# A gather that fetches four experts for 32 tokens each, summed in four 32-column groups of TensorE

## The reference

```
def block(xb):                                   # 128 tokens
    q = (xb @ w_pq).reshape(PEER_BLOCK, 8, 2, 128)
    s1 = einsum('thk,nk->thn', q[:, :, 0], sub_keys1)
    s2 = einsum('thk,nk->thn', q[:, :, 1], sub_keys2)
    v1, i1 = top_k(s1, 16);  v2, i2 = top_k(s2, 16)
    cand = v1[..., :, None] + v2[..., None, :]
    sc, ci = top_k(cand.reshape(..., 256), 16)
    e = i1[ci // 16] * 128 + i2[ci % 16]         # 8 heads x 16 = 128 experts a token
    g = softmax(sc, axis=-1)
    u = peer_u[e];  v = peer_v[e]                # rows of 1024 from 16384 experts
    a = gelu(einsum('td,thkd->thk', xb, u))
    return einsum('thk,thkd->td', g * a, v)
...
ple = sigmoid(h @ w_ple_gate) * (p @ w_ple)
y = layer_norm(2 ** 0.25 * h + ffn + ple, ln2_g, ln2_b)
```

## Time and profile before

| | |
|---|---|
| Median of 3 timed runs | 2196.86 us (2189.36 to 2201.34) |
| Span of the profiled execution | 2204.2 us (no time of its own is given; 0.3% above the median) |
| TensorE busy | 1901.9 us, 86%; weight loads 46% |
| VectorE / ScalarE / GpSimd busy | 61% / 29% / 34% |
| Gathers | 576, 604.02 MB, 67.5% of the 16 DMA engines' span |
| Chain that ended last | PE 47%, DMA 22%, DVE 15%, issue 8% |

### The profile page before, as it was taken

How to read it: one execution, slowest core, us unless ns; L and a number is a source line. 1 busy time by engine, 2 the same in 40 slices (tenths; PEclk the granted TensorE clock), 3 DMA queues, 4 the chain that set the end, 5 groups by cost and what they waited for, 6 DMA issues and landing times.

```text
span 2204.2 us, 22373 instructions
## 1 busy us (share of the span) xinstructions
PE 1901.9 (86%) x7052; PEld 1015.8 (46%) x7052; DVE 1350.5 (61%) x3200; ACT 642.5 (29%) x2012; POOL 753.1 (34%) x784
## 2 busy tenths in 40 slices
PE   8988899999988988889989988859797979788775
PEld 6577666565454544454445444424343333333221
DVE  3339961122878888888788878853545554444554
ACT  0012221120133333333333333323333333233332
POOL 0001117000044344334443446544443443444442
PEclk9988989999999999899989999979999999999999
DMA  7010035656099999999999999999999999999996
GB/s 291 9 43 1 1 131 229 262 200 265 1 383 400 386 365 393 383 377 362 392 384 385 355 384 383 405 417 361 386 382 405 372 408 385 413 379 379 419 421 285
DMA packets 99331, 693.41 MB, mean 315 GB/s; under 512 B 11105, under 2 KB 15841, under 8 KB 22177
## 3 DMA queue, kind: packets, MB, share of 16 engines
q0 software_dynamic: 82944, 604.02, 67.5%
q1 hardware_dynamic: 16288, 88.15, 10.5%
HBM read 686.96 MB, written 4.87 MB: 314 GB/s over the span
## 4 chain that ended last, share of the span: by engine, by line
PE 47%; DMA 22%; DVE 15%; issue 8%; POOL 4%; ACT 3%; POOLq 0%; SPq 0%; ACTq 0%; DVEq 0%
DMA R<-d_uv,E 21%; PE bank L878 16%; PE bank L845 5%; DVE R L1591 5%; PE bank L574 4%; POOL R L535 4%; PE bank L718 3%; PE bank L686 3%; PE bank L789 3%; PE bank L826 3%; PE bank L568 2%; DMA W<-d_pT 1%; PE bank L623 1%; DVE E L1521 1%; DVE E L1524 1%
## 5 line engine op out<-in xcount | busy, mean ns | idle before, releaser
L878 PE MATMUL bank<-R,E 128*128 128x512 f32 (+1 forms) x2304 | 1082.2, 624 | 234.2 <-ACT E L1149 234.0
L535 POOL DMA_INDIRECT R<-d_uv,E x576 | 684.4, 1188 | 1104.9 <-PE bank L878 595.9
L1591 DVE CUSTOM_DVE_ANT_0 R<-R,E 128x1024 f32<-128x1024 f32 x576 | 694.0, 1223 | 458.0 <-DMA R<-d_uv,E 456.4
L878 PEld LDWEIGHTS bank<-R,E 128*128 128x128 f32 (+1 forms) x2304 | 431.5, 193 | 853.6 <-issue 507.0
L1149 ACT ACTIVATE E<-ident,E 128x128 f32<-128x128 f32 x512 | 177.6, 394 | 8.4
L1141 ACT ACTIVATE E<-E 128x2 f32<-128x2 f32 x288 | 57.9, 201 | 380.9 <-DVE E L1591 380.5
L845 PEld LDWEIGHTS bank<-E,W 128*128 128x128 f32 x1280 | 145.9, 192 | 10.8 <-issue 9.4
L845 PE MATMUL bank<-E,W 128*128 128x128 f32 (+1 forms) x1280 | 146.1, 275 | 1.1 <-ACT E L1080 1.1
L1144 ACT ACTIVATE E<-E 128x1 f32<-128x1 f32 x576 | 138.2, 287 | 13.2 <-ACT E L1141 1.7
L1120 ACT COPY E<-E 128x4 uint32<-128x4 uint32 (+1 forms) x146 | 27.8, 191 | 340.5 <-DVE E L1591 335.0
L574 PE MATMUL bank<-E,W 128*128 128x288 f32 x384 | 95.9, 413 | 8.3 <-DMA E<-d_xT 8.3
(11 more groups left out here) (277 smaller groups left out, 1655.5 us busy)
## 6 DMA issues: line engine op xcount, KB each, us to landing
R<-d_kc SPq DMA_DIRECT2D x8, 2560.0 KB, 9.3
R<-d_vc SPq DMA_DIRECT2D x8, 2560.0 KB, 8.6
R<-d_uv,E POOLq DMA_INDIRECT x576, 10.9
W<-d_w_pq SPq DMA_DIRECT2D x4, 2048.0 KB, 12.8
W<-d_w_in SPq DMA_DIRECT2D x3, 2048.0 KB, 15.6
R<-d_w_out SPq DMA_DIRECT2D x2, 2048.0 KB, 7.9
W<-d_w_gate SPq DMA_DIRECT2D x2, 2048.0 KB, 13.7
E<-d_xT SPq DMA_DIRECT2D x2, 1152.0 KB, 8.0
```

What stands on the lines that cost most here:

```text
L535: pool.indirect_dma_start(ring[r], None, A["uv"], bass.IndirectOffsetOnAxis(ap=stage[:, half, s:s + 1], axis=0),).then_inc(landed[r], 16)
L878: last = mm(acc[:, half * 512:half * 512 + 512], diag[:, r, 0:m], ring[r][:, D + half * 512:D + half * 512 + 512], start=False, stop=True, ...
L1591: last = nc.vector.tensor_tensor_reduce(ring[r][:, 0:D], ring[r][:, 0:D], hS[:, b, :], 1.0, 0.0, ALU.mult, ALU.add, dots[:, x, s:s + 1])
```

## The change

A gather now takes four experts of 32 tokens instead of one expert of 128 tokens. Partition 32s + t holds an expert of token 32j + t, where j, the token group, is the slot's number modulo four (modulo two in the last block). There are still 576 gathers of 128 rows.

- `h` is laid out anew for each block: `hrep[32s + t, j]` is `h` of token 32j + t, repeated for s = 0 to 3. It is filled by 16 DMAs from SBUF to SBUF of 32 x 4 KB each, 2 MB together (8 for the last block). For block 0 SyncE issues them, for the later blocks ScalarE does (`spread_h`), after its last half-turn of the block before. VectorE waits for them (`in_hrep`) at a block's first dot.
- Expert numbers and weights come out of `resolve` in a small buffer `eg`. ScalarE moves them to the new layout by 16 copies a pick (`lay`, 8 in the last block).
- The diagonals become 128x32 (`wsel`, `fold` scaled by partition). TensorE waits once a half-turn, for all four, then does the first 512 columns of the four slots, then the second 512; slot r goes to rows 32j of the accumulator, that is, to another group of 32 columns of the array. The four slots are marked free with the last four matmuls.
- `rows2` (1 MB) is loaded with the gate's weights, not ahead of the gathers. The copies to the upper partitions for the last block are gone.

```diff
+TG = 32
+SG = P // TG
...
+        if n >= 2:
+            order.append(("lay", *picks[n - 1]))
...
+    experts(1)
+    order.append(("lay", *picks[-1]))
...
-        diag = view(E, 0, RING, P)
-        rows2 = view(E, 1024, 2, D)
-        keep = view(E, 3072, D)
-        alpha_id = view(E, 4096, P)
+        wsel = view(E, 0, RING, TG)
+        hrep = view(E, 256, SG, D)
+        alpha_id = view(E, 4352, P)
...
-            load(rows2, A["rows2"], in_rows2)
+            sp.wait_ge(h_ready, 1)
+            for j in range(SG):
+                for s in range(SG):
+                    load(hrep[TG * s:TG * s + TG, j, :], hS[TG * j:TG * j + TG, 0, :], in_hrep)
...
-            sp.wait_ge(h_ready, BLOCKS)
-            sp.dma_start(hS[ST:P, QB, :], hS[0:ST, QB, :]).then_inc(hdup, 16)
-            sp.wait_ge(picked, 4 * BLOCKS)
-            c0 = QB * EXP
-            sp.dma_start(eall[ST:P, c0:c0 + 64], up_e[0:ST]).then_inc(packed, 16)
-            sp.dma_start(gall[ST:P, c0:c0 + 64], up_g[0:ST]).then_inc(packed, 16)
...
+            load(rows2, A["rows2"], in_rows2)
...
+                groups = m // TG
+
                 def half_turn(i, x):
-                    for r in range(HALF * x, HALF * x + HALF):
-                        pe.wait_ge(diagonal, i * RING + (r + 1))
-                        for half in range(2):
-                            last = mm(acc[:, half * 512:half * 512 + 512], diag[:, r, 0:m],
+                    pe.wait_ge(diagonal, i * RING + (HALF * x + HALF))
+                    for half in range(2):
+                        for r in range(HALF * x, HALF * x + HALF):
+                            p0 = TG * (r % groups)
+                            last = mm(acc[p0:p0 + TG, half * 512:half * 512 + 512], wsel[:, r, :],
                                       ring[r][:, D + half * 512:D + half * 512 + 512],
                                       start=False, stop=True, skip_group_check=True)
-                        last.then_inc(slot_free, 1)
+                            if half == 1:
+                                last.then_inc(slot_free, 1)
 
                 turns(pe, h0, h1, half_turn)
 
...
+            def lay(b, c):
+
+                _, m = tokens_of(b)
+                groups = m // TG
+                act.wait_ge(picked, 4 * b + c + 1)
+                for j in range(groups):
+                    for s in range(SG):
+                        c0 = b * EXP + 8 * c * groups + j
+                        last = nc.scalar.copy(egall[TG * s:TG * s + TG, :, c0:c0 + 7 * groups + 1:groups],
+                                              eg[TG * j:TG * j + TG, :, 8 * s:8 * s + 8])
+                last.then_inc(laid, 1)
+
+            def spread_h(b):
+
+                _, m = tokens_of(b)
+                act.wait_ge(h_ready, b + 1)
+                for j in range(m // TG):
+                    for s in range(SG):
+                        act.dma_start(hrep[TG * s:TG * s + TG, j, :], hS[TG * j:TG * j + TG, b, :]).then_inc(in_hrep, 16)
 
             def experts(h0, h1):
 
...
-                            f(diag[:, x * HALF + s, 0:m], sel[:, 0:m], ACT.Copy,
+                            f(wsel[:, x * HALF + s, :], fold[:, :], ACT.Copy,
                               scale=wts[:, x, s:s + 1]).then_inc(diagonal, 1)
 
                 turns(act, h0, h1, half_turn)
+                if h1 * HALF == (b + 1) * EXP and b < QB:
+                    spread_h(b + 1)
...
-            act.wait_ge(picked, 1)
+            lay(0, 0)
+            act.wait_ge(laid, 1)
...
-                link(stt(efl[0:m], e12[0:m, 0, :], float(NKEY), e12[0:m, 1, :], ALU.mult, ALU.add))
+                if n >= 1:
+                    dve.wait_ge(laid, n)
+                stt(eg[0:m, 0, :], e12[0:m, 0, :], float(NKEY), e12[0:m, 1, :], ALU.mult, ALU.add)
...
-                if h0 * HALF == QB * EXP:
-                    dve.wait_ge(hdup, 16)
+                _, m = tokens_of(b)
+                groups = m // TG
+                if h0 * HALF == b * EXP:
+                    dve.wait_ge(in_hrep, 16 * SG * (SG * b + groups))
...
-                            ring[r][:, 0:D], ring[r][:, 0:D], hS[:, b, :], 1.0, 0.0, ALU.mult, ALU.add,
+                            ring[r][:, 0:D], ring[r][:, 0:D], hrep[:, r % groups, :], 1.0, 0.0, ALU.mult, ALU.add,
...
-    a["fold"] = np.tile(np.eye(ST, dtype=np.float32), (2, 1))
+    a["fold"] = np.tile(np.eye(TG, dtype=np.float32), (SG, 1))
```

More of the change, by code:

```diff
@@ L195, in build @@
         ident = sb("ident", [P, P])
-        fold = sb("fold", [P, ST])
+        fold = sb("fold", [P, TG])
         iota = sb("iota", [P, PK])
@@ L227, in build @@
         oh = view(E, 14592, 2 * PK, PK)
-        gall = view(E, 15616, STEPS + RING)
-        eall = view(E, 16208, STEPS + RING).bitcast(U32)
+        egall = view(E, 15616, 2, STEPS + 2 * RING)
         tv = view(E, 16800, 4, PK)
@@ L237, in build @@
         e12 = view(E, 17184, 2, 2 * PK)
-        efl = view(E, 17248, 2 * PK)
         gx = view(E, 17280, 2, PK)
         gsm = view(E, 17312, 2)
-        up_e = view(E, 17316, 4 * PK).bitcast(U32)
-        up_g = view(E, 17380, 4 * PK)
+        eg = view(E, 17316, 2, 2 * PK)
         dots = view(E, 19008, 2, HALF)
@@ L246, in build @@
         stage = view(E, 19032, 2, HALF).bitcast(U32)
-        diag = view(E, 0, RING, P)
-        rows2 = view(E, 1024, 2, D)
-        keep = view(E, 3072, D)
-        alpha_id = view(E, 4096, P)
+        wsel = view(E, 0, RING, TG)
+        hrep = view(E, 256, SG, D)
+        alpha_id = view(E, 4352, P)
+        keep = view(E, 17444, D)
         keysT = view(E, 19040, 2, NKEY)
@@ L291, in build @@
         sgm = view(Wf, 2 * 4096 + 3200, 512)
-        gp = view(Wf, 3 * 4096, 4, D)
+        gp = view(Wf, 3 * 4096, 2, D)
+        rows2 = view(Wf, 3 * 4096 + 2048, 2, D)
         asc = view(Wf, 12032, CT, ST)
@@ L340, in build @@
             sem(n) for n in ("pq_full", "pq_ready", "s_full", "s_ready", "s_used"))
-        gx_ready, gexp_done, picked, packed = (sem(n) for n in ("gx_ready", "gexp_done", "picked", "packed"))
-        hdup = sem("hdup")
+        gx_ready, gexp_done, picked, laid = (sem(n) for n in ("gx_ready", "gexp_done", "picked", "laid"))
+        in_hrep = sem("in_hrep")
         staged, granted, slot_free, dotted, gelued, weighed, diagonal = (
@@ L1119, in copy_stage @@
             def copy_stage(half, at):
-                return nc.scalar.copy(stage[:, half, :], eall[:, at])
+                return nc.scalar.copy(stage[:, half, :], egall[:, 0, at])
+            def lay(b, c):
[14 more added lines that the diff above has]
+                        act.dma_start(hrep[TG * s:TG * s + TG, j, :], hS[TG * j:TG * j + TG, b, :]).then_inc(in_hrep, 16)
             def experts(h0, h1):
                 b = block_of(h0)
-                _, m = tokens_of(b)
-                sel = ident if b < QB else fold
                 if (h1 + 1) * HALF < QB * EXP:
-                    act.wait_ge(picked, (h1 + 1) * HALF // (2 * PK) + 1)
+                    act.wait_ge(laid, (h1 + 1) * HALF // (2 * PK) + 1)
                 else:
-                    act.wait_ge(picked, 4 * BLOCKS)
-                    act.wait_ge(packed, 32)
+                    act.wait_ge(laid, 4 * BLOCKS)
                 def half_turn(i, x):
@@ L1144, in half_turn @@
                             last = f(wts[:, x, s:s + 1], gel[:, x, s:s + 1], ACT.Copy,
-                                     scale=gall[:, column(i, x * HALF + s, 1)])
+                                     scale=egall[:, 1, column(i, x * HALF + s, 1)])
                         last.then_inc(weighed, 1)
@@ L1179, in _ @@
             parts = {"turn": turn, "ask_out": ask_out, "match_out": match_out, "cross": cross,
-                     "experts": experts, "gate_turn": gate_turn, "gate_out": gate_out, "finish": finish}
+                     "lay": lay, "experts": experts, "gate_turn": gate_turn, "gate_out": gate_out, "finish": finish}
             for what, *at in ORDER:
@@ L1601, in gate_out @@
                 dve.wait_ge(gate_sig, 2 * b + half + 1)
-                tt(gp[0:m, b % 4, half * 512:half * 512 + 512], sgm[0:m], bank[0:m, 3 - 2 * half, :],
+                tt(gp[0:m, b % 2, half * 512:half * 512 + 512], sgm[0:m], bank[0:m, 3 - 2 * half, :],
                    ALU.mult).then_inc(gate_used, 1)
@@ L1618, in finish @@
                 dve.wait_ge(gate_used, 2 * b + 2)
+                if b == 0:
+                    dve.wait_ge(in_rows2, 16)
                 if b >= 1:
@@ L1621, in finish @@
                 if b == 0:
-                    link(tt(ybuf[0:m], keep[0:m], gp[0:m, b % 4, :], ALU.add))
+                    link(tt(ybuf[0:m], keep[0:m], gp[0:m, b % 2, :], ALU.add))
                 else:
-                    tt(ybuf[0:m], sum_of(b), gp[0:m, b % 4, :], ALU.add).then_inc(acc_used, 1)
+                    tt(ybuf[0:m], sum_of(b), gp[0:m, b % 2, :], ALU.add).then_inc(acc_used, 1)
                     dve.wait_ge(acc_used, b + 1)
```

12 lines of the change are left out of this document (2 added, 10 removed).

## The result

The changed kernel takes 2382.14 us (median of 4 runs, 2377.86 to 2388.35); the kernel before took 2195.91 on the same chip (2189.36 to 2201.34). The forecast was 2228 us, with 2165 to 2280 as its range. The sign and the place of one loss were right; the size was not, and the term that was to be a gain, the picks, was a loss.

The account below looks back on a forecast made before the run. The prediction took a ring of engines and gather DMA, each waiting for the next, as the bound. Picks -40, edges +60, start +6, `rows2` +2.5, gates and last block +3 gave 2235.7, scaled to 2228 us; range 2165 to 2280.

Parts of the forecast that it names:

- The column groups: TensorE's half-turn: four 32-column groups overlap fully, 1.7 us at full clock or 3.4 at the low one, from 6.9.
- The rival without overlap: Column groups don't run side by side at 512 columns; a half-turn keeps 6.9 us: 2304 us, chance 0.08.
- The standstills behind each `ask`: In the picks: the DMA's 2.4 us standstill, main place of 4.5 us lost a pick, would mostly go.
- I charge 0.5 us for each, 2 us: Picks: the first two slots return about 5 us later, leaving a shallow DMA queue four times a pick; cost 2 us.
- the prediction's own sign of being wrong: Picks staying at 44 us, the shallow queue eating the gain, where 41 to 43 us was forecast without an edge.
- +3: Gates and last block: gates hold TensorE as before, the last block has two column groups; +3 us (-10 to +15).
- My range for the picks: Bounds on the picks' forecast gain of 40 us: from nothing to 81 us gained.
- 512 packets take 14.9 us: Edge between blocks: the copies of `h` alternate packets with the gathers, at 34 packets per us.
- the forecast's 11.3: Full edge between blocks: 11.3 us DMA standstill plus 5.0 of transfer; all four edges together +60 us.
- The start: Block 0's copies go with the first gathers, first dot at 627 where it was 616.23; +6 us (2.5 to 11).
- The clock: TensorE's clock in the picks falls to 0.6 or so; up to 2 us lost where an `ask` starts low.
- `lay` and the smaller weights: The 16 copies a pick cost 0 under cover, up to 48 us without; smaller weights save ScalarE about 0.1 us each.

Follow-up runs that it names:

- the kernel kept busy: Changed kernel plus six zero-weight matmuls in each half-turn of the picks not behind an `ask`: 2362.9 us, 1.075 of before.
- slot by slot: Changed kernel, but TensorE waits for each slot's weights and frees each slot after its two matmuls: 2246.3 us, 1.021 of before.
- the best one: Changed kernel with a wait and release per slot, `h` repeated by TensorE for blocks 1 to 4, and zero-weight matmuls in the picks: 2162.6 us, 0.981 of before.
- slot by slot with no copies: Changed kernel with a wait and release per slot and no `h` copies for blocks 1 to 4 (result wrong): 2172.2 us, 0.987 of before.

## Why the prediction was wrong in size and right in sign

The steps that failed are two terms of the sum: the 0.5 us for each half-turn given back together, and the pace of the copies, 34 packets per us. The sign of the whole came right in part by luck: the forecast had a gain in the picks, where the kernel lost, and a loss at the edges alone.

**The column groups: right.** 16 instructions took 3.64 us at 1.2 GHz (0.50), the forecast's 3.4 and the tail, and 1.92 us at 2.4 GHz in the kernel kept busy, its 1.7 and the tail. The price of going from 32-column to 128-column weights, which the prediction left open, is small: at 2.4 GHz the first matmul behind a half-turn starts 522 ns after its last one in the kernel kept busy, and 429 ns before, where both have 128 columns. The rival without overlap (chance 0.08) is refuted by that, though its 2304 us lies nearer to the result than mine.

**The standstills behind each `ask`: right, but worth less.** From 700 to 940 the kernel before has five stretches of 0.7 to 1.7 us in which no packet moves, 5.6 us in all; the changed kernel has 0.2 us. The share went from 0.94 to 0.97. But that is about 1 us a pick: the 4.5 us a pick by which the ring was behind didn't go mainly there, as the prediction read it.

**"I charge 0.5 us for each, 2 us": wrong, and the largest miss.** The step said that the first two slots of a half-turn come back 5 us later, and priced it at 0.5 us by feel, in the picks alone. A pick stayed where the prediction's own sign of being wrong had it: at 376 GB/s 16 gathers take 44.6 us, slot by slot (402 GB/s) 41.7. The difference between the changed kernel and slot by slot is 0.79, 0.79, 0.76 and 0.80 us a half-turn in the four blocks and 1.71 in the last one, 106 us between the edges and 24 in them. Two parts of that were missed. In the gates' stretch and the last block ("+3") a half-turn pays as well; there I charged nothing. And the price could be bounded from rows, which I do here after the fact and as an estimate: eight slots given back four at a time leave four gathers to the DMA, 4 x 2.49 = 10.0 us. The way from the fourth dot to the next landing was 1.6 (ScalarE) + 3.4 (TensorE) + 0.8 (GpSimd) + 7.4 from issue to dot = 13.2 us. The ring is up to 3.2 us a half-turn too short, so up to 461 us over 144 half-turns. The measured 130, 0.9 us a half-turn, is a quarter of that. With TensorE's 6.9 us for the kernel before the same count gives 6.7 us a half-turn, and the measured 242 us are 1.7, a quarter again; why only a quarter is open. My range for the picks (nothing to -81) held no loss.

**The gain without that charge.** Slot by slot has 47 us less than before between the edges. The forecast had (4.5 - 0.3) x 18 = 76 less 5.5. Same sign, smaller.

**"512 packets take 14.9 us": the premise failed.** The place, the idle VectorE and the standstill behind it came as foretold: VectorE stands from 995 to 1022, 27 us and not 13 to 21, and the DMA stands for 12 us, the forecast's 11.3. But the copies ran at 19 packets per us. The 34 per us came from a store of `y`, which reads all 128 partitions. When the copies write 128 partitions, they run at 38 and the dot comes 19.0 us after the first issue, the forecast's 19.3. Even the standstill is smaller there than the 11.3 us of the forecast, the share of 0.20 over 9 us:

```profile
999.00:1008.00 9.00, 5.15 (x16) 2.13 (x16) 8.47 (x25) 5.06 (x24) 0.72 (x1) 0.50 0.20 84
```

and the four edges cost 37 us over before, where I had 60. Since each copy of the changed kernel writes 32, its edges cost 96. Of these, 24 belong to the grouped release: slot by slot they cost 72. The issue on ScalarE (10.2 us for 16) lay beside the transfer, as assumed; four issues in 1.8 us in place of 16 brought 9 us in all.

**The start: +17, not +6.** The copies for block 0 write 32 partitions as well. VectorE's first dot comes at 637.55 and not 627, after 19.6 us of idle time that ends with them:

```profile
609.62 10.31 SPq L366 DMA_DIRECT2D E<-E  x16
...
637.55 1.23 DVE L1613 CUSTOM_DVE_ANT_0 R<-R,E 128x1024 f32<-128x1024 f32 x1 [19.62 <-DMA E<-E]
```

**The clock.** It fell, to 0.69 in the picks (816 to 1303.5) where the forecast had 0.6 or so, and to 0.75 over the span. Keeping TensorE busy in the picks gives back 19 us in the changed kernel and 18 in the best one (2180.9 against 2162.6, two chips; by their ratios 0.991 and 0.981). I had counted only what it does to the 1.7 us of the half-turn and up to 2 us at an `ask`.

**`lay` and the smaller weights: nothing seen.** In slot by slot with no copies, which has `lay`, "between" is 44 us under before; no cost of it shows beside that. It was not tried alone.

## What to carry to other kernels

In a ring of slots, count what is left in flight while a group is held: slots not in the group, times the pace, against the whole way from the last one's arrival to the next landing. If the first is shorter, batching a wait can cost up to the difference at each turn (here a quarter of it, 0.9 of 3.2 us and 1.7 of 6.7), even where it shortens the work itself. And price a copy from a row that touches as many partitions, not only one of the same packet size; a layout that many small copies must build may be cheaper on an engine that has just been relieved.

## What the runs showed that I had not expected

- Copies that each write 32 partitions move 19 packets of 4 KB per us beside gathers, and slow these to 477 ns a packet; with 128 partitions 38 and 315 ns.
- At a share near full the DMA's rate still differs: 376 GB/s at 0.97 in the changed kernel, 402 at 0.99 slot by slot. By the share alone the latter at 0.97 would be 394. So most of the 26 GB/s is in how long packets take, not in idle engines, when the slots come back four at a time. From 700 to 940 the gathers' packets have a median of 309 ns in both, and a mean of 336 against 323: some packets take much longer. Why is open, and no run takes it apart.
- Zero-weight matmuls that bring the clock from 0.83 to 0.90 over the span make the best kernel 1% faster, though from 700 to 940 the chain of work that ended last had 34% in the gathers' DMA and 10% in TensorE's half-turns.
